# Second mixer: the pooling's running sums move from VectorE to GpSimd, and two weight splits move later on VectorE

## The reference, cut to what matters

```python
h = _rmsnorm(x, pre_norm_g[l])
proj = jnp.einsum('btd,de->bte', h, w_in[l])
q_a, f_a, i_a, g_a, u_b, g_b, q_c, k_c, v_c, g_c, f_c = jnp.split(proj, IN_SPLIT_POINTS, axis=-1)
f_gate = lb + (1.0 - lb) * jax.nn.sigmoid(f_a)
log_f_a = jnp.log(jnp.maximum(f_gate, TINY))
k_a = (1.0 - lb) * jax.nn.sigmoid(-f_a)
o_a = _hgrn2_chunkwise(silu(q_a), k_a, i_a, log_f_a)      # chunks of 64 tokens here
pooled = _multiscale_pool(u_b)                            # windows 2, 4, 8, 16 by group of 64 channels
o_b = jnp.einsum('btgc,gcd->btgd', pooled, pool_w[l]) * pool_scale[l] * silu(g_b)
log_f_c = jax.nn.log_sigmoid(f_c + fox_f_bias[l])
o_c = _forgetting_attention(q_c, k_c, v_c, log_f_c) * silu(g_c)
x = x + _rmsnorm(jnp.concatenate([o_a, o_b, o_c], -1) @ w_out[l], post_norm_g[l])
...
def _multiscale_pool(u):
    for g, w in enumerate(POOL_WINDOWS):
        count = jnp.minimum(t + 1.0, float(w))
        outs.append((upper - lower) / count - uf[:, :, g])   # mean of the last w tokens, less the token
```

## Time and profile before

| what | us |
|---|---|
| median of three runs | 1862.21 |
| lowest and highest run | 1858.18, 1864.83 |
| the profiled execution, its own time | 1864.81 |
| its span, first to last instruction | 1863.1 |
| in it: PE busy | 1800.2 |
| DVE busy | 1284.9 |
| ACT busy | 974.6 |
| POOL busy | 156.7 |

### The profile page before, as it was taken

The page is one execution under the profiler, slowest core; times in us unless marked ns, Lnnn a source line. Parts: engine busy times, 40 slices in busy tenths (PEclk is TensorE's granted clock), DMA queues, the critical chain, the costliest instruction groups (busy, mean ns, idle before and its releaser), DMA issues. The chain is left out here.

```text
span 1863.1 us, 33639 instructions
## 1 busy us (share of the span) xinstructions
PE 1800.2 (97%) x13010; PEld 1646.4 (88%) x13010; DVE 1284.9 (69%) x2275; ACT 974.6 (52%) x1811; POOL 156.7 (8%) x175
## 2 busy tenths in 40 slices
PE   7999999899899999999999999999999998999998
PEld 7999999799689999999999967789888886788776
DVE  6769889886653877777766266597777766974554
ACT  6557864567752744444444257375444444434772
POOL 1115441000000000000000011000000003000101
PEclk8999999999999999999999999999999999999999
DMA  8223471245342233332232232323323232322101
GB/s 202 76 81 126 132 211 48 75 133 173 98 110 84 69 97 109 93 110 91 91 92 91 71 89 72 91 70 114 112 90 113 91 105 79 92 91 63 52 23 46
DMA packets 209652, 179.60 MB, mean 96 GB/s; under 512 B 42544, under 2 KB 181808, under 8 KB 209512
## 3 DMA queue, kind: packets, MB, share of 16 engines
q1 hardware_dynamic: 209512, 177.68, 32.5%
HBM read 164.10 MB, written 13.54 MB: 95 GB/s over the span
## 5 line engine op out<-in xcount | busy, mean ns | idle before, releaser
L196 PE MATMUL ps<-ffn_alo,main_whi 128*128 128x264 f32 (+1 forms) x768 | 205.7, 322 | 0.0
L196 PE MATMUL ps<-ffn_ahi,main_wlo 128*128 128x264 f32 (+1 forms) x768 | 205.1, 321 | 0.0
L196 PE MATMUL ps<-ffn_ahi,main_whi 128*128 128x264 f32 (+1 forms) x768 | 204.7, 321 | 0.0
L196 PE MATMUL ps<-gdn_xhi,gdnf_whi 128*128 128x264 f32 x768 | 157.2, 286 | 4.2 <-DVE gdnf_wlo L1568 4.2
L500 DVE TENSOR_TENSOR main_wlo<-raw,main_whi 128x512 fp32r<-128x512 f32 x212 | 145.0, 686 | 18.8 <-ACT main_whi L389 9.2
L562 DVE TENSOR_TENSOR h<-h,ps 128x528 f32<-128x528 f32 (+1 forms) x128 | 89.1, 696 | 98.7 <-PE ps L196 98.0
L196 PE MATMUL ps<-gdn_xlo,gdnf_whi 128*128 128x264 f32 x768 | 155.9, 284 | 0.0
L196 PE MATMUL ps<-gdn_xhi,gdnf_wlo 128*128 128x264 f32 x768 | 155.9, 284 | 0.0
L165 DVE TENSOR_TENSOR main_wlo<-raw,main_whi 128x2048 fp32r<-128x2048 f32 x38 | 88.2, 2320 | 81.4 <-ACT main_whi L158 81.4
L196 PEld LDWEIGHTS ps<-ffn_ahi,main_whi 128*128 128x128 f32 x768 | 127.8, 188 | 11.2
L196 PEld LDWEIGHTS ps<-ffn_ahi,main_wlo 128*128 128x128 f32 x768 | 127.5, 188 | 10.9
(11 more groups left out here) (554 smaller groups left out, 4851.4 us busy)
## 6 DMA issues: line engine op xcount, KB each, us to landing
raw<-in_ff_up_dram SPq DMA_DIRECT2D x32, 1024.0 KB, 5.5
raw<-in_ff_down_dram SPq DMA_DIRECT2D x32, 1024.0 KB, 5.0
raw<-in_gdn_in_dram SPq DMA_DIRECT2D x24, 1024.0 KB, 5.7
raw<-in_w_in_dram SPq DMA_DIRECT2D x14, 1024.0 KB, 5.4
raw<-in_mlstm_in_dram SPq DMA_DIRECT2D x12, 1024.0 KB, 5.3
raw<-in_gdn_out_dram SPq DMA_DIRECT2D x8, 1024.0 KB, 6.6
gdn_zr<-gdn_z_spilled SPq DMA_DIRECT2D x26, 264.0 KB, 3.1
gdn_v_spilled<-gdn_o SPq DMA_DIRECT2D x16, 264.0 KB, 2.3
```

The lines of the kernel that those rows point to most:

```text
L196: mm = pe.matmul(ps[:, b, 0:k.width], w, x[:, half], start=first and n == 0, stop=last and n == 2)
```

## The change

It moves the sums of `Pooling` from DVE to POOL. `pooling.dve` is parted in two: `counts` stays on DVE (nine small instructions, counted in a new semaphore `counted`), and `windows` runs on POOL, behind its mask fills and ahead of its wait for `nb`. There it waits for `counted` and for the first two tiles' copies. The scaling by 1 / win and the subtraction, one `scalar_tensor_tensor` on DVE, are two instructions on POOL. On DVE, `split(3)` and `split(5)` are now issued behind what `beside` does at their hooks, where before they were ahead of it. ACT, PE and SP keep their order.

```diff
-    def dve(self, k, dve, left):
-        u, a, c, cnt, head = self.u, self.a, self.c, self.cnt, self.head
-        link = linked(dve, self.chain)
-        dve.wait_ge(left, 2)
-        link(dve.memset(u[:, :, 0:S0], 0.0))
-        link(dve.memset(a[:, :, 0:S0], 0.0))
-        link(dve.memset(c[:, :, 0:S0], 0.0))
+    def counts(self, dve):
+        cnt, link = self.cnt, linked(dve, self.counted)
         dve.wait_ge(self.count, 1)
...
+    def windows(self, pool, left):
+        u, a, c, cnt, head = self.u, self.a, self.c, self.cnt, self.head
+        link = linked(pool, self.chain)
+        for x in (u, a, c):
+            link(pool.memset(x[:, :, 0:S0], 0.0))
+        pool.wait_ge(self.counted, 2 * len(WINDOWS) + 1)
+        pool.wait_ge(left, 2)
+
         src, dst = u, a
         for g, win in enumerate(WINDOWS):
...
-                link(dve.tensor_tensor(dst[r, j, S0:T], src[r, j, S0:T], src[r, j, S0 - d:T - d], ALU.add))
+                link(pool.tensor_tensor(dst[r, j, S0:T], src[r, j, S0:T], src[r, j, S0 - d:T - d], ALU.add))
...
-            link(dve.scalar_tensor_tensor(out=v[r, j, S0 + META:T], in0=v[r, j, S0 + META:T], scalar=1.0 / win,
-                                          in1=u[r, j, S0 + META:T], op0=ALU.mult, op1=ALU.subtract))
-            link(dve.tensor_tensor(v[r, j, S0:S0 + META], head[r, j, :], u[r, j, S0:S0 + META], ALU.subtract))
+            link(pool.tensor_scalar(v[r, j, S0 + META:T], v[r, j, S0 + META:T], 1.0 / win, None, ALU.mult))
+            link(pool.tensor_tensor(v[r, j, S0 + META:T], v[r, j, S0 + META:T], u[r, j, S0 + META:T], ALU.subtract))
+            link(pool.tensor_tensor(v[r, j, S0:S0 + META], head[r, j, :], u[r, j, S0:S0 + META], ALU.subtract))
 
         for j in range(2):
-            dve.tensor_copy(a[HW:P, j, S0:T], c[HW:P, j, S0:T]).then_inc(self.pooled, 1)
+            pool.tensor_copy(a[HW:P, j, S0:T], c[HW:P, j, S0:T]).then_inc(self.pooled, 1)
...
             pool.wait_ge(s.masks, n + 1)
+            pooling.windows(pool, s.left)
             pool.wait_ge(s.nb_in, 16 * FH)
...
                     lower_bounds()
-                    pooling.dve(k, dve, s.left)
+                    pooling.counts(dve)
                     gates.dve(k, dve, 1)
...
             for j, x in hooks:
-                if x == 2 and j < FOX0 and not HGRN_FIRST[0] <= j < HGRN_FIRST[1]:
+                if x == 2 and j < FOX0 and j not in (3, 5) and not HGRN_FIRST[0] <= j < HGRN_FIRST[1]:
                     split(j)
                 beside(j, x)
+                if x == 2 and j in (3, 5):
+                    split(j)
```

More of the change, by code:

```diff
@@ L3634, in open @@
         self.cnt_i, self.cnt = sb("cnt_i", [P, META], mybir.dt.int32), sb("cnt", [P, 2, META])
-        self.w_zero, self.w_in, self.sc_in, self.count, self.chain, self.pooled, self.mixed, self.out = (
-            k.sem(f"pl_{x}") for x in ("w_zero", "w_in", "sc_in", "count", "chain", "pooled", "mixed", "left"))
+        self.w_zero, self.w_in, self.sc_in, self.count, self.counted, self.chain, self.pooled, self.mixed, self.out = (
+            k.sem(f"pl_{x}") for x in ("w_zero", "w_in", "sc_in", "count", "counted", "chain", "pooled", "mixed", "left"))
     def group(self, g):
@@ L3671, in dve @@
                 r = slice(0, P) if 2 * j >= g else slice(HW, P)
-                link(dve.tensor_tensor(dst[r, j, S0:T], src[r, j, S0:T], src[r, j, S0 - d:T - d], ALU.add))
+                link(pool.tensor_tensor(dst[r, j, S0:T], src[r, j, S0:T], src[r, j, S0 - d:T - d], ALU.add))
             r, j = self.group(g)
-            link(dve.tensor_tensor(head[r, j, :], dst[r, j, S0:S0 + META], cnt[r, j, :], ALU.mult))
+            link(pool.tensor_tensor(head[r, j, :], dst[r, j, S0:S0 + META], cnt[r, j, :], ALU.mult))
             if g < 3:
```

## The result

| | before | changed |
|---|---|---|
| median of six runs, us | 1862.11 | 1887.38 |
| lowest and highest | 1858.18, 1864.83 | 1879.01, 1894.10 |
| the profiled execution: own time, span | 1864.81, 1863.1 | 1887.80, 1886.1 |
| mean granted clock of the profiled execution | 0.988 | 0.981 |

The changed kernel is slower: ratio 1.0129, 95% interval 1.0114 to 1.0144. The forecast was 1882.3 in a range of 1875 to 1890.

The account below looks back on a forecast made before the run. PE's stream and its waits were taken to bound the kernel (busy 1800.2 of 1863.1 us). Tile 6 10.6 us late, tile 8 later still, less the transposes' give-back, left tile 9 20.1 late: 1862.2 + 20.1 = 1882.3, range 1875 to 1890.

Parts of the forecast that it names:

- Pooling off DVE gives 0.75 us: Ahead of the gates' second-mixer activations: of 10 us of DVE work freed, only 0.75 us reach the chain.
- Tile 6 late by 10.6: Second mixer: split of unit 3 behind forget() makes tile 6 start at 1618.6 instead of 1608.01, 10.6 us PE idling.
- GpSimd's chain 23.8 us: Pooling sums on GpSimd from about 1588.1: instruction times sum to 23.8 us, so pooled is there at 1611.9.
- It hides behind the split: At the pooled matmuls: PE's 5 us wait for GpSimd lies within the wait for unit 3, costing nothing, 0.3 at worst.
- Tile 8 late by 22.3 through tile 7 and ACT: Tile 8's split waits for the level, that for ACT's exponentials, these for tile 7: start 1643.3 instead of 1621.04.
- The remark in brackets: Before tile 8: the logarithm behind tile 6, scans and differences take less than tile 7 and ACT's work, so are hidden.
- The give-back at the transposes, and one cold restart for each wait: Tile 8 to tile 9: transposes' 2.65 us wait and 1.7 of clock go; each long wait adds a 2.2 us restart.
- No slack later: After tile 9 of the second mixer: no later slack, so the end moves by the same 20.1 us.
- (a): Rival, second mixer: faster, two waits and the clock behind them go, - 5.5 us to 1856.7; 3 in 100.
- (b): Rival: only tile 6's loss, the level done within tiles 6 and 7; 7.3 us late, 1869.5; 6 in 100.
- (c): Rival: GpSimd and DVE hinder each other on the chain, 5.2 us instead of 0.5; 24.8 late, 1887.0; 10 in 100.

Follow-up runs that it names:

- e5: Kernel before with pooling on GpSimd, both splits ahead, pooled matmuls one tile later, `pooling.act` behind ACT's logarithm; 1862.57 us against 1863.20, ratio 0.9995.
- e2: Kernel before with only the two splits moved, pooling staying on DVE; 1885.67 us against 1863.47, ratio 1.0123.
- e7: Changed kernel with ACT's exponentials ahead of its copy of tile 7 and split of unit 5; 1881.58 us against 1862.31 for the kernel before.
- e3: Kernel before with only the split of unit 3 moved behind forget(), pooling on DVE; 1871.44 us against 1863.47, ratio 1.0049.
- e6: e5 with ACT's three activations of the gates one tile earlier; 1860.46 us against 1863.20 for the kernel before, ratio 0.9988.
- the second: Second set of runs of the changed kernel itself, unaltered, against the kernel before; 1884.47 us against 1863.20, ratio 1.0116.

## Why the prediction was right, step by step

- **Pooling off DVE gives 0.75 us.** Right: DVE idles 11.29 us ahead of L3751, which starts 0.9 us earlier than before against the copy of tile 0, and e5 shows that the move as a whole is worth nothing.
- **Tile 6 late by 10.6.** It was 11.4. The term that was too small is what GpSimd's work beside DVE costs: I took 0.5 of a bound of 0 to 5.2. In the rows the scan L3755 took 2.17 instead of 1.21, and the two scalings L4109 1.50 instead of 1.01; from the scan's start to the end of forget() 15.82 us against 14.38, so 1.4. The 0.9 that was too little there, less 0.2 that the first step gave more, is the 0.8.
- **GpSimd's chain 23.8 us.** It was 23.7, but that is luck: the terms were off and cancelled. The scalings took 1.45 to 1.47 and not 0.98, more than the subtraction with two inputs (1.25); the additions 1.04 to 1.29; the small ones 0.22 where nothing stood in the way, not 0.63, and one 1.67 beside DVE's instructions.
- **It hides behind the split.** Right, as e2 shows: without GpSimd the wait is 10.3, and it is 4.4 + 4.4 with it, the matmuls between them.
- **Tile 8 late by 22.3 through tile 7 and ACT.** It was 22.3, and the order of the chain was the one named: copy, split, exponentials right behind one another. The exact number is luck: tile 6 was 0.8 later than forecast, but tiles 6 and 7 took 13.5 us where 14.1 was forecast, and from tile 7's end to L4129 it was 4.4 and not 4.6. e7 shows that this link decides, but that only 2 to 3 us hang on it. The remark in brackets, that the logarithm behind tile 6 and the scans are hidden, is right by no more than that; it passes over the link from tile 6 through ACT's logarithm, on which, by the rows, the other 8 us of the wait hang.
- **The give-back at the transposes, and one cold restart for each wait.** Right: the transposes do not wait, and tile 9 is late by 19.8 for 20.1. The granted clock was 0.50 for 4.1 us behind tile 6's wait, that is 1.2 GHz. The restarts cost 1.7 us (tiles 6 and 7, 13.5 against 11.9) and 1.9 (tile 8 to tile 9, 10.6 against 8.7), each a little under the 2.2.
- **No slack later.** Right: 229.0 us from tile 9 to the end in both.
- **Rivals.** (a) fell with the three waits. (b), only the first loss, fell with the wait of 10.4 at tile 8; as a kernel of its own, e3, it gives about what (b) was worth, + 8.0 by the medians and + 9.2 by tile 9, against 7.3. (c) was there at 1.4 us and not at 5.2 in the changed kernel; in e6, where forget() starts earlier and more of it lies beside GpSimd's chain, it is 3.2. So the first set's median of 1887.38, which is (c)'s 1887.0, does not speak for (c).
- The median came 5 us over the sum in the first set and 1 us over in the second. No step has this: in the one profile of the first set 3.2 us lie ahead of the mixer's tiles, most of it from one stretch of low clock. The forecast held this only as the scatter of the kernel before, 1858 to 1865.

The Trainium skill (SBUF — State Buffer, two separate sides) has GpSimd and a VectorE instruction with two SBUF inputs or in a two-port mode hold a shared port one at a time. The rows agree for short instructions (1.75 for 0.67, and 1.67 for 0.22 on GpSimd's side). The reciprocal, with one input, took 6.55 us in every kernel, with GpSimd busy beside it or not.

## What to carry to other kernels

A weight split that seems to be in the way of a long chain may be covered by tensor work in progress; before it is moved behind the chain, compare the end of the chain with the first matmul that wants the weights. Where each engine keeps its own order, work taken off an engine is worth only what its next wait allows: here ten us freed gave 0.9, since the next instruction waited for three activations of another engine, and moving those three was worth more than moving the ten. Two delays in a row do not simply add: ask whether the second one starts from the first. Here it did, because an engine's copy of a late tile stood ahead of a logarithm that did not need that tile.

## What the runs showed of the hardware that was not expected

GpSimd's scaling of 64 x 496 float32 took 1.45 us, more than its subtraction of the same size with two inputs (1.25). GpSimd's and VectorE's short instructions hold each other up: forget() took 13.25 us alone and 16.40 beside GpSimd's chain. And the scatter of one kernel differs from set to set: the changed kernel's six runs spread over 15 us (mean clock 0.977 to 0.987) and four others over 2.3 us (0.983 to 0.984); the kernel before spread over 6.7 us in six runs and 15.8 in 21 (0.981 to 0.992).
